# Gated delta rule: the 32x32 diagonal blocks of the prompt chunks inverted by VectorE in front of the chunk loop

## The reference

```python
gc = cumsum(g)                                       # within a chunk
decay = exp(where(incl, gc_i - gc_j, -inf))
A = where(strict, (k @ k.T) * decay * beta, 0)
sol = triangular_solve(eye + A, [v * beta, k * beta * exp(gc)], lower, unit_diagonal)
P = (q @ k.T) * decay
# per chunk, in order:
U = w_v - w_k @ S
o = (q * exp(gc)) @ S + P @ U
S = S * exp(g_last) + (k * exp(g_last - gc)).T @ U
```

## Time and profile before

| | |
|---|---|
| median of 3 runs | 1697.13 us (1695.96 to 1700.67) |
| the profiled execution | 1700.1 us, span 1698.3 us |
| TensorE busy | 98% of the span |
| VectorE, ScalarE, GpSimd busy | 70%, 41%, 23% |
| opening | until 231.7 us |
| delta stage, periods 0 to 8 | from 233.0 to 418.0 us |
| spread(1), spread(2), spread(3), spread(8) on TensorE | 254.26, 273.54, 293.13, 391.07 us |

### The profile page before, as it was taken

One profiled execution on the slowest core, in us unless ns is written; L12 is line 12 of the kernel. 1 busy time (PEld: TensorE's weight loads), 2 busy tenths in 40 slices (PEclk: granted clock), 3 DMA queues, 4 the chain that ended last, 5 costly groups with the idle time before them and its releaser, 6 DMA issues.

```text
span 1698.3 us, 25734 instructions
## 1 busy us (share of the span) xinstructions
PE 1661.0 (98%) x10233; PEld 1554.7 (92%) x10233; DVE 1195.0 (70%) x1612; ACT 703.7 (41%) x1306; POOL 398.8 (23%) x377
## 2 busy tenths in 40 slices
PE   6999999999999999999989999999999999999998
PEld 6999999999999999999977889999988888999987
DVE  5687536765655857445832598888889878777787
ACT  5222224454343333341312565555554444444444
POOL 1011343344145656453551300000003000000001
PEclk9999999999999999999999999999999999999999
DMA  6012212001877676779854155555553555455543
GB/s 201 26 56 60 80 54 62 2 2 32 294 253 227 196 233 223 253 252 376 271 180 161 50 160 183 184 191 188 186 186 104 171 161 158 153 162 162 176 158 125
DMA packets 212579, 269.67 MB, mean 159 GB/s; under 512 B 9930, under 2 KB 168855, under 8 KB 212460
## 3 DMA queue, kind: packets, MB, share of 16 engines
q1 hardware_dynamic: 175928, 219.48, 40.4%
q10 hardware_dynamic: 35892, 45.39, 7.9%
q0 software_dynamic: 640, 3.15, 0.5%
HBM read 211.95 MB, written 56.04 MB: 158 GB/s over the span
## 4 chain that ended last, share of the span: by engine, by line
PE 54%; DMA 18%; POOL 7%; DVE 4%; issue 1%; SPq 1%; ACT 1%; POOLq 0%; DVEq 0%; ACTq 0%
PE ps L3447 19%; PE ps L3476 18%; DMA ff_sums<-ff_prep 9%; DMA ff_prep<-in_w_up 5%; DMA ff_prep<-in_w_down 4%; PE ps L3388 4%; PE ps L3459 2%; PE ps L1432 2%; PE ps L1455 1%; POOL ff_prep L1989 1%; POOL ff_prep L1987 1%; POOL ff_prep L1998 1%; POOL ff_prep L1985 1%; POOL ff_prep L1992 1%; POOL ff_prep L1994 1%
## 5 line engine op out<-in xcount | busy, mean ns | idle before, releaser
L3092 DVE TENSOR_TENSOR w_lo<-ff_raw,w_hi 128x1024 fp32r<-128x1024 f32 x225 | 275.8, 1232 | 71.3 <-ACT w_hi L2878 71.1
L2878 ACT CAST w_hi<-ff_raw 128x1024 fp32r<-128x1024 f32 x225 | 233.7, 1052 | 159.8 <-PE ps L3476 122.9
L3447 PE MATMUL ps<-x_half,w_hi 128*128 128x320 f32 (+1 forms) x832 | 194.1, 304 | 1.5 <-ACT hid L2917 1.5
L2482 PE MATMUL ps<-xn_hi,g_hi 128*128 128x384 f32 x464 | 156.7, 338 | 0.8 <-issue 0.4
L2482 PE MATMUL ps<-xn_hi,g_lo 128*128 128x384 f32 x464 | 155.2, 334 | 0.0
L2482 PE MATMUL ps<-xn_lo,g_hi 128*128 128x384 f32 x464 | 155.2, 334 | 0.0
L3447 PE MATMUL ps<-x_half,w_lo 128*128 128x320 f32 (+1 forms) x512 | 155.0, 303 | 0.0
L3447 PEld LDWEIGHTS ps<-x_half,w_hi 128*128 128x128 f32 x832 | 142.2, 189 | 2.7 <-issue 1.9
L3197 DVE TENSOR_TENSOR rows<-ps,rows 128x512 f32<-128x512 f32 x210 | 136.0, 680 | 2.6 <-PE ps L3476 1.8
L1918 DVE TENSOR_TENSOR g_lo<-g_raw,g_hi 128x512 fp32r<-128x512 f32 x91 | 72.8, 806 | 87.5 <-ACT g_hi L1913 87.3
L3476 PE MATMUL ps<-w_hi,hid_hi 128*128 128x512 f32 x280 | 110.7, 395 | 0.6
(11 more groups left out here) (393 smaller groups left out, 4265.0 us busy)
## 6 DMA issues: line engine op xcount, KB each, us to landing
ff_raw<-ff_sums SPq DMA_DIRECT2D x120, 512.0 KB, 3.8
ff_sums<-ff_prep SPq DMA_DIRECT2D x60, 512.0 KB, 5.0
ff_raw<-in_w_down SPq DMA_DIRECT2D x57, 512.0 KB, 4.3
ff_raw<-in_w_up SPq DMA_DIRECT2D x48, 512.0 KB, 3.8
ff_prep<-in_w_up SPq DMA_DIRECT2D x32, 512.0 KB, 4.6
ff_prep<-in_w_down SPq DMA_DIRECT2D x56, 256.0 KB, 3.4
g_raw<-in_w_in ACTq DMA_DIRECT2D x22, 512.0 KB, 6.4
gates<-gate ACTq DMA_DIRECT2D x16, 576.0 KB, 6.4
```

The source lines that it names most:

```text
L2482: last = nc.tensor.matmul(out, a[:, w_of(c)], x(c), start=(start and n == 0 and m == 0), stop=(stop and n == len(ks) - 1 and m == 2), skip ...
L2878: nc.scalar.copy(hi[slot(t, j)][:, :], raw_of(t, j)).then_inc(hi_done, 1)
L3092: nc.vector.tensor_tensor(lo[s][:, :], raw_of(t, j), hi[s][:, :].bitcast(F32), ALU.subtract).then_inc(lo_done, 1)
L3447: last = nc.tensor.matmul(ps[:, PROD_BANK[i] + m, 0:w], y[s][:, at], x[g][i][:, k], start=(NEW[i] and k == 0 and n == 0), stop=(k == 3 and ...
```

## The change

Levels 0 to 4 of the eight prompt chunks go. In their place the 32x32 diagonal blocks of all chunks and heads (8 x 4 x 4 = 128 blocks) are gathered so that each block lies in one partition, and VectorE inverts them all at once by elimination. Levels 5 and 6 stay on TensorE; level 5 now multiplies only the 32x32 blocks. In the opening TensorE makes k k^T of every prompt chunk once more (`diagonal_products`, between the units of tiles 9 and 10), ScalarE copies the diagonal blocks out (`keep_products`), GpSimd and ScalarE make the decays. VectorE scales and transposes (behind tiles 9 and 10 and in the first z block) and runs elimination steps 1 to 4, 5 to 8, 9 to 14 among the z gates, steps 15 to 30 in period 0 of the delta stage. Each instruction of this chain waits for the one before it. SyncE then copies the inverted blocks into the lanes' `ti`, four DMAs a chunk, of which those of chunks 2 to 7 go out as lanes get free; the loads of the stream states now stand between and behind these. z keeps one buffer in place of two. The order of all engines in a period is written anew. Cut to its core:

```diff
+        def solve_step(dve, ins):
+            n_solving[0] += 1
+            ins.then_inc(solving, 1)
+            dve.wait_ge(solving, n_solving[0])
+        def eliminate(dve, first, last):
+            for j in range(first, last + 1):
+                n = QP - 1 - j
+                part = inv_part[:, 0:n * j].rearrange("p (i c) -> p i c", c=j)
+                below = inv_rows[:, j + 1:QP, 0:j]
+                solve_step(dve, nc.vector.tensor_tensor(part, inv_rows[:, j + 1:QP, j:j + 1].to_broadcast([P, n, j]),
+                                                        inv_rows[:, j:j + 1, 0:j].to_broadcast([P, n, j]), ALU.mult))
+                solve_step(dve, nc.vector.tensor_tensor(below, below, part, ALU.add))
...
+                        for n in {(9, 1): (0,), (9, 2): (1, 2), (10, 0): (3,), (10, 1): (4, 5), (10, 2): (6, 7)}.get((tile, g), ()):
+                            keep_products(n)
+                    if tile == 10:
+                        act.wait_ge(solving, 2)
+                        nc.scalar.activation(decay[:, :, :], decay[:, :, :], ACT.Exp).then_inc(decay_made, 1)
...
+                    if made[0] == 9:
+                        nc.gpsimd.tensor_tensor(decay_in[:, :, :], per_slot(gc_slots), before, ALU.add).then_inc(decay_begun, 1)
...
+                    if tile == 9:
+                        solve_step(dve, nc.vector.transpose(squared_off(decay), squared_off(decay_in)))
+                        solve_step(dve, tt_(decay[:, :, :], decay[:, :, :], per_slot(gc_slots), ALU.subtract))
+                    if tile == 10:
+                        solve_step(dve, tt_(inv_rows[:, :, :], inv[:, :, :], same, ALU.mult))
+                        solve_step(dve, vv.tensor_reduce(inv_sum[:, :], inv_rows[:, :, :], mybir.AxisListType.X, ALU.add))
+                        solve_step(dve, tt_(inv[:, :, :], inv[:, :, :], decay[:, :, :], ALU.mult))
...
                     for g in range(NT):
                         z_gated(dve, f, g)
+                        if f == 2 and g < 2:
+                            eliminate(dve, 9 + 3 * g, 11 + 3 * g)
+                    if f == 1:
+                        eliminate(dve, 5, 8)
+                    if f == 0:
+                        solve_step(dve, ts_(inv_sum[:, :], inv_sum[:, :], 4 * EPS, None, ALU.add))
+                        solve_step(dve, vv.reciprocal(inv_beta[:, :], inv_sum[:, :]))
+                        solve_step(dve, tt_(inv_beta[:, :], beta_slots, inv_beta[:, :], ALU.mult))
+                        solve_step(dve, tt_(inv[:, :, :], inv[:, :, :], per_slot(inv_beta), ALU.mult))
+                        solve_step(dve, tt_(inv[:, :, :], same, inv[:, :, :], ALU.subtract))
+                        solve_step(dve, vv.transpose(inv_rows[:, :, :], inv[:, :, :].rearrange("p s c -> p c s")))
+                        eliminate(dve, 1, 4)
...
+                        for n in {(9, 0): (0,), (9, 1): (1, 2), (9, 2): (3,), (10, 0): (4, 5), (10, 1): (6,), (10, 2): (7,)
+                                  }.get((tile, g), ()):
+                            diagonal_products(n)
...
+                    for q in range(4):
+                        sp.dma_start(b["ti"][quarter(q), :, quarter(q)], self.inverse.blocks[quarter(q), n * H:(n + 1) * H, :]
+                                     ).then_inc(s["t0"], 16)
```

More of the change, by code:

```diff
@@ L56 @@
 LEVELS_S = 4
+QP = P // 4
 M_TAIL = 3 * (1 + STREAMS)
@@ L707, in unit, with diagonal_products @@
                         last.then_inc(unit_done, 1)
+                def diagonal_products(n):
+                    if n == 0:
+                        pe.wait_ge(out_done, 2 * 2 * H)
+                    if n >= 3:
+                        pe.wait_ge(kk_kept, 4 * (n - 2))
+                    kk = ps[:, KK_BANKS[n % 3], :].rearrange("p (h c) -> p h c", c=P)
+                    keys = self.qkv[:, H:2 * H, n * P:(n + 1) * P]
+                    for f in range(H):
+                        last = nc.tensor.matmul(kk[:, f, :], keys[:, f, :], keys[:, f, :], start=True, stop=True)
+                    last.then_inc(kk_made, 1)
                 def first_part(tile, g, part):
@@ L1002, in _ @@
                 for period in PERIODS:
-                    B, old = period, period - 2
+                    B, A, old = period, period - 1, period - 2
+                    if 0 < A < SAMPLE:
+                        state_decay(A)
                     if valid(old):
@@ L1128, in _ @@
                     if valid(A):
-                        taken(A, 5)
-                    if valid(old):
-                        back(old)
-                    grown(B)
-                    if valid(A):
                         turned(A)
+                    if B in (0, SAMPLE):
+                        grown(B)
                     if B == 0:
@@ L1308, in _ @@
                     scaled_keys(B)
-                    decayed(B)
-                    factors(B)
-                    if valid(A):
-                        turned(A, 5)
-                        masked(A, 5)
-                    first(B)
-                    queries(B)
-                    if B == 0:
-                        last_z.gated(dve, 0)
-                        last_z.gated(dve, 1)
                     if A > 0:
                         rest(A)
-                    masked(B, 1)
+                    decayed(B)
                     if valid(A):
                         masked(A, 6)
-                    values(B)
+                    if B == SAMPLE:
+                        factors(B)
+                    else:
+                        queries(B)
                     if valid(A):
                         solved(A)
-                    turned(B, 2)
-                    masked(B, 2)
+                    if B == SAMPLE:
+                        first(B)
+                        queries(B)
+                    if B == 0:
+                        factors(B)
+                        for g in range(NT):
+                            last_z.gated(dve, g)
+                    values(B)
+                    if B == SAMPLE:
+                        masked(B, 1)
                     if valid(A):
                         weighted(A)
-                    turned(B, 3)
+                    if 0 < B < SAMPLE:
+                        factors(B)
                     if valid(B + 1):
                         key_norms(B + 1)
-                    masked(B, 3)
+                    if B == SAMPLE:
+                        turned(B, 2)
+                        masked(B, 2)
                     if valid(A):
                         carry(A)
-                    if B == 0:
-                        last_z.gated(dve, 2)
-                    turned(B, 4)
+                turned(SAMPLE, 3)
+                masked(SAMPLE, 3)
                 merging.rest(dve, 0)
@@ L1599, in _ @@
                     if valid(A):
                         level_end(A, 6)
-                    level_begin(B, 2)
-                    if valid(B + 1):
-                        turn_keys(B + 1)
-                    else:
+                    turn_values(B)
+                    if B == SAMPLE:
+                        level_begin(B, 1)
+                    if valid(A):
+                        solve(A)
+                        state_part(A)
+                    if B == SAMPLE:
+                        level_end(B, 1)
```

275 lines of the change are left out of this document (158 added, 117 removed).

## The result

The changed kernel takes 1675.72 us (median of four runs, 1674.32 to 1678.49); the kernel before took 1696.55 beside it (1694.15 to 1700.67). The ratio is 0.9877, 95% interval 0.9852 to 0.9901. Forecast: 1675.0. The profiled execution took 1677.03 us with a span of 1675.0.

What follows compares the result with a forecast made beforehand. TensorE, busy 98% of the span, bounds the kernel; +17.1 + 1.6 - 7.8 + 2 - 34.2 - 0.8 = -22.1 us takes the profiled 1700.1 to 1678.0, less 3.0 to the median: 1675, range 1660 to 1688.

Steps and rivals of the forecast that it cites:

- Opening, +17.1: Stage before the delta periods: 7.1 diagonal products, 7.7 stall, 2 clock and 0.3 late VectorE work lengthen it by 17.1 us.
- The stall 7.7: Opening: TensorE stands 7.7 us because VectorE's short steps wait for GpSimd's x sums; bounds 0 to 1 and 10.
- rival A: Opening: short VectorE steps slip between GpSimd's sums, saving 8.7 us of stall and clock; total 1666; chance 0.18.
- The clock's 2: Opening: half granted clock after TensorE's stall costs 2 us, bounds 0 and 2.5.
- Period 0, +1.6: First delta period: VectorE's elimination steps 15 to 30 make it 22.9 against 21.3 us; bounds -3 and +6.
- Period 1, -7.8 + 2: Second delta period: 11.5 against 19.28 us, -7.8, plus 2 for half clock after period 0's idle.
- Steady period, 13.9: Delta periods 2 to 7: 13.9 against 19.59 us each, -34.2 in all; bounds 12.4 and 15.5 a period.
- level 5 ... no gain: Steady period: level 5 keeps its 16 short matmuls on smaller operands and is given no gain.
- Rival C: Steady period held at 15.5 us by a ring from GpSimd's strict and decayed_keys to turn_keys; total 1685; chance 0.15.
- Rival B: Steady period hits its 12.4 us floor of TensorE slots if rest(A) came in time; total 1666; chance 0.10.
- Stream period, -0.8: Period with the stream groups: loses chunk 7's level 4 (1.78), gains waits: -0.8 of 26 us; bounds -2 and +2.
- Rival D: Elimination's short rows and dependent waits cost far more, 0.8 us an instruction: +26, total 1701; chance 0.05.

Runs made afterwards that it cites:

- the second trace: Trace of the changed kernel run again unaltered, the base of the other runs: 1676.94 us, ratio 0.9877 to the kernel before.
- the run without sums: Changed kernel with GpSimd's convolution sums from the 13th on replaced by 4-element memsets; reference not computed: 1666.27 us, ratio 0.9815.
- the first trace: Trace of the changed kernel's first measurement, with a clock of 0.91 over 40 to 60 us: median 1675.72 us, profiled execution 1677.03.
- full rows: Changed kernel with level 5's first product group on all 128 operand rows instead of 32; reference not computed: 1678.00 us, ratio 0.9884.
- the block moved whole: Changed kernel with the opening block's first 14 VectorE instructions behind z block 1's gates instead of block 0's: 1678.22 us, ratio 0.9881.
- the last kernel: Changed kernel with split opening block, next chunk's keys turned later, 18 dummy products ending TensorE's opening and 36 in period 0: 1658.18 us, ratio 0.9773.
- the run beside it without fillers: Changed kernel with split opening block and next chunk's keys turned later, no dummy products: 1666.74 us, ratio 0.9810.
- both sets of fillers: Changed kernel with 27 unread dummy products ahead of the waiting z product group and 30 in period 0: 1667.71 us, ratio 0.9823.
- the block split: Changed kernel with the opening block's first six instructions left in place, elimination steps 1 to 4 moved behind z block 1's gates: 1671.52 us, ratio 0.9849.

## Why the prediction was right, step by step

The mechanism held at every step that the runs could try. The sum was close partly because errors of both signs cancelled: up to chunk 8, 4.7 us too little was forecast as gain (steady periods 3.7, stall 0.6, period 1 at full clock 0.4) and 3.0 too much (the two half clocks 0.9 and 1.3, period 0 0.8).

**Opening, +17.1.** Measured +17.2 in the second trace. The diagonal products: the tail transposition behind them starts at 210.2 there and 203.1 before, exactly the 7.1.

```profile
203.13 1.47 PE L780 MATMUL ps<-con,tail_q 128*27 128x128 f32 x12
```

The block began at 215.9 in the second trace (forecast 216.0) and ended at 232.0 (forecast 232.3). The stall 7.7 was 7.12 and 7.13; rival A (no turn-taking) is excluded, and the run without sums, 1666.3, has about the time that A gave. The clock's 2 was 2.4 and 2.9: from the tail transposition to chunk 0 TensorE takes 30.4 us before, 30.5 without the sums and 40.5 in the second trace, of which 7.1 is the stall. So 7.1 + 7.1 + 2.9 and 0.1 of a longer wait at the end give the 17.2, where the forecast had 7.1 + 7.7 + 2 + 0.3. The Trainium skill (SBUF — State Buffer, "SBUF: two separate sides") calls the port pair that GpSimd shares with a VectorE instruction of two SBUF inputs an exclusive lock for the whole instruction; 2.33 us for what costs 0.21 alone agrees, and the one-input transposition and the copy out of the sum banks, unchanged beside the sums, agree too. Mis-sized: the block alone was 7.6 us and not 6.8, because its 1024-element transposition is 2.08 and not some 1.4, as I had also priced the way back. It is not the length: a transposition of as many elements earlier in the opening, with its operands in stored order and not rearranged from "p s c" to "p c s", takes 1.24. That the rearrangement is the reason is likely, but no run varies it.

```profile
182.08 1.24 DVE L724 STREAM_TRANSPOSE decay<-decay_in 128x1024 f32<-128x1024 f32 x1
```

**Period 0, +1.6.** Measured +2.4 (23.16 for 20.78). TensorE's idle time was forecast at 8.6 and is 8.59; the elimination ended at 268.14. What I had short was for the most part again the transposition back, 1.99 for 1.4.

**Period 1, -7.8 + 2.** At full clock it is 11.10 (forecast 11.5), -8.2; the half clock costs 3.1 and 3.4 there in the two traces of this kernel. The base's sum is -4.8, the first trace's -5.1, against -5.8.

**Steady period, 13.9, "level 5 ... no gain".** This is the largest mis-sized term: 13.27, so -37.9 in place of -34.2. TensorE's first group of level 5 holds it 0.37 us, not the 0.7 of my walk; with full rows it is 0.62. The Trainium skill (TensorEngine Tiling (Array Packing), "Key Properties") says that different tiles of the array can load weights and multiply in parallel; the 0.37 against 0.62 and the starts in pairs agree. With 0.37 in the walk the period would have been about 13.6. The stall before the keys was 0.78 for 1.1, the one before the values 0.17 for 0.25; with these too the walk gives 13.2. Rival C (15.5, a ring over GpSimd) is out: in the steady periods neither TensorE nor VectorE waits for GpSimd. Rival B did not happen in this order; its floor of 12.4, in which level 5 still stood with 0.7, is passed (12.23) when one transposition is moved.

**Stream period, -0.8.** From the spread of chunk 8 to the stage's last transposition of queries it is 25.47 for 26.26: -0.8.

**Rival D, elimination steps of 0.8 us.** Start to start they are 0.22 us at 30 elements (267.73 to 267.95 in the first trace) and 0.44 at 240, which is what the formula gave.

**The balance.** Chunk 8 was forecast at -21.3 (the sum without the stream period), and is -23.2 in the second trace, -21.5 in the first: the better steady period against dearer clock passages and the transpositions. To the end of the execution the second trace gains 25.0 and the first 23.3. The medians differ by 20.8 and 21.6: the profiled execution of the kernel before was a long one, as the 3.0 us in the prediction allowed for.

## What to carry to other kernels

Where one engine was full, its slots gave the gain to about a tenth (34.2 forecast, 37.9 measured), but the work moved to another engine must be priced on that engine's own calendar: small VectorE instructions with two SBUF inputs cost up to a whole GpSimd instruction each beside the sums (0.21 us became 1.9 to 2.3), so they belong where GpSimd is idle and the large ones into VectorE's gaps. When a stage gets shorter, look again at its order: the transposition that now stood 0.78 us too early cost 6 us over the stage. A move that takes away a stall is priced by both engines' ends, not by the stall (the block moved whole gained nothing, split it gained 5).

## What the hardware showed that I had not expected

A hole in TensorE costs half clock besides itself, and not the same each time. Four traces with the keys in their old place have the hole of 8.6 us in period 0, and period 1 takes 13.24 (full rows), 14.16, 14.45 and 16.54 us (without the sums) for 11.10 at full clock: 2.1 to 5.4 us more, though period 1 runs the same program but for the full rows. Products that nobody reads give it back: in the last kernel the granted clock is 1.00 from 240 to 300 us and the run beside it without fillers is 8.6 us slower, 2.4 of it by chunk 8. Filling most of a hole can merely move the fall: with 2.0 us of wait left period 1 was 13.87 in one run and 12.42 in the other, with 0.7 left 11.48 (in the order with the keys later, where it was 13.06 without fillers).

Executions of the same instructions differ by single holes. The clock fell between 40 and 60 us in four of the twelve traces of the changed kernel and its variants (they are 2.4 to 2.7 us behind the second trace by 60 us), and one wait far behind the changed part, TensorE's for the scaled rows, was 6.15 us in the first trace of the changed kernel, 7.58 in the second, 11.46 with the block split and 4.94 in the last:

```profile
870.32 1.97 PE L3510 MATMUL ps<-con,scaled 128*128 128x128 f32 x8 [6.15 <-DVE scaled L3244]
```
```profile
869.09 1.97 PE L3510 MATMUL ps<-con,scaled 128*128 128x128 f32 x8 [7.58 <-DVE scaled L3244]
```

So part of the last kernel's 8.6 us, and of the 9.2 us with both sets of fillers, lies in the stages behind, where the kernels are alike. The three traces with fillers have the three shortest of these waits (4.94, 5.23 and 5.46 us; the other nine 6.15 to 11.46) and the shortest way from chunk 8 to the end (1301.7 to 1303.4 us for 1305.4 to 1310.5). An earlier arrival does not explain it, since runs without fillers arrive earlier than two of them. What does, no run here settles.
